# Feed-forward down stage: operand loads issued from ScalarE's step loop instead of SyncE's

## The chip, the cores and the metric

One Trainium2 chip, one core of it. The metric is the device time of one execution in microseconds (us), here the median of the runs of the same program.

## What is computed

One layer of a streaming encoder for 1152 tokens (1024 of a prompt, 8 x 16 of a sample), all in float32. The layer is: a half-step SwiGLU feed-forward network (`ffn`, called "f1"), a combined projection, sparse attention and an mLSTM branch with an output projection, and a second half-step SwiGLU network ("f2"), then a final norm. The change lies in `ffn` alone, which computes

```
a, b = split(rmsnorm(x, g) @ w_up)
x + 0.5 * ((silu(a) * b) @ w_down)        # D_MODEL 1024, D_FF 2816
```

and runs twice, once with each network's weights. Outputs that matter here are `y_prompt` and `y_sample`; the other outputs (keys, values, mLSTM state) do not depend on anything that is changed.

## The kernel before, in words

The program is written by hand for each engine: TensorE multiplies, ScalarE and VectorE evict and form operands, GpSimd forms the low halves of weights, SyncE issues every DMA. Every float32 product is three passes over split values (`product3`, L515: hi weight with lo activation, lo with hi, hi with hi), and every 2x2 block product of `ffn` is done with seven products instead of eight.

`ffn` (L522) is divided into tiles `n`: 22 up tiles (`UPS`) and 20 down tiles (`DOWNS`), and each tile into steps `q` (8 for the first two tiles, else 7). Steps are numbered through by `step(n, q)`: the up stage is steps 0 to 155, the down stage 156 to 295. TensorE (L1034 and on) takes one product per step, adds one to the semaphore `mm_ok` when it is done, and works through the steps in order. A step of the down stage has 12 matmuls of 288 columns (18 in the last round).

The activations between the stages don't fit in the on-chip memory as they are needed. For each pair of up tiles (a group `g`, eleven of them), seven combinations are split into hi and lo in a small ring of three staging buffers `stg` and stored to the DRAM tensor `h_dram`. ScalarE makes the hi half (`pack_hi`, L798), VectorE the lo half (`pack_lo`, L969), SyncE stores it (`store`, L721), and ScalarE may fill a staging buffer again only when its last store has landed (L805). The seven packs of the last group fall in steps 151 to 161, so across the border of the stages.

The down stage reads them back. It has five rounds of four tiles; round `r` works on the groups `ROUNDS[r]` (two groups, three in the last round), and its seven operands `xd[r, q]` are each loaded whole by `load_operand(r, q, s)` (L703), one DMA of 576 KB per group. A table `LOAD_AT` (L577) says at which step a load stands in the program: round 0 at steps 150 to 153 (two operands at 150, 151 and 152, one at 153), first used at steps 156 to 162; later rounds one operand every three steps through the round before, with first use 22 to 28 steps after (round 1: steps 156, 159, 162, and so on, first use 184 and on); the last three operands of the last round, with three DMAs each, at 262, 263 and 265, first use 272, 273 and 274. A load waits for `mm_ok` to reach its last argument (the step that freed the memory it overwrites), for the same operand of the round before, and for the stores of the groups that it reads.

What orders the other engines at each step `s`:

- SyncE (L729 to L737): raw weights for a later tile (`load_raw`, L692, which waits for GpSimd's progress on weights), then stores, then operand loads, then a residual load. It has no wait per step: it goes through the list and stops only where one of these calls waits.
- ScalarE (L853 to L857): `evict` (up stage only), then `split_hi` (L744) of the weight slot that this step frees, which waits until TensorE is done with step `s`, then `rest` (L821), in which `pack_hi` stands. A weight slot that is split at step `s` is multiplied at step `s + 4`; there are four slots.
- GpSimd (L867): the lo half of each weight slot, after the hi half.
- VectorE (L984 on): `evict`, which in the down stage is `accumulate` (L908: a PSUM pair added into `xT`), then `pack_lo`, `combine` (L954), and the differences of weights (`weight_term`, L875). TensorE may use a PSUM bank again only after `accumulate` has emptied it (`free_bank`): for step 160 that is the accumulation of step 158.

Of the kernel before, what the change touches and what calls it, by code (L numbers as in the profile page):

```python
# [16 lines left out]
F32 = mybir.dt.float32  # L17
# [504 lines left out]
def ffn(nc, ctx, M, K, w_up, w_down, gain, xT, xT_at, places, h_dram, r_dram, tag, first, last_io=None):  # L522

    sem = lambda n: ctx.enter_context(nc.semaphore(tag + n))
    UPS, ROUNDS = 2 * NG, ((0, 1), (2, 3), (4, 5), (6, 7), (8, 9, 10))
    DOWNS, RING, STG = 4 * len(ROUNDS), 4, 3
# [5 lines left out]
    def step(n, q):  # L532
        return 8 * n + q if n < 2 else 16 + 7 * (n - 2) + q

    def slot_no(n, x):
        return 4 * n + x if n < 2 else 8 + 7 * (n - 2) + x
# [35 lines left out]
    LOAD_AT = {}  # L572
    for r in range(len(ROUNDS)):
        for q in range(7):
            at, size = OPERAND[r, q]
            s = max(u[2] for u in used if u[0] < at + size and at < u[0] + u[1])
# [4 lines left out]
    done_groups = lambda r: sum(len(x) for x in ROUNDS[:r + 1])  # L581

    with ExitStack() as mem, M.scope():
# [13 lines left out]
             for x in range(3)]  # L597
# [8 lines left out]
        xd = {(r, q): M.at(f"{tag}xd{r}{q}", [P, len(ROUNDS[r]), 2, HT], OPERAND[r, q][0], F32R)  # L606
              for r in range(len(ROUNDS)) for q in range(7)}
        ps = psum(nc, mem, tag + "ps", [P, 8, 512])
        w_in = [sem(f"w_in{x}") for x in range(2)]
        st = [sem(f"st{x}") for x in range(STG)]  # L610
        xd_in = [sem(f"xd_in{q}") for q in range(7)]
# [11 lines left out]
        def round_of(n):  # L623
            return ROUNDS[(n - UPS) // 4]

        def raw_of(n):
            if n < UPS:
                return raw_u[:, n % 2].rearrange("p (k n) -> p k n", k=KT)
            return raw_d[:, n % 2, 0:len(round_of(n)) * 4 * P].rearrange("p (k n) -> p k n", n=2 * P)
# [51 lines left out]
        def y_block(m, i):  # L681
            k, t = 2 * (m % 4) + (0, 1, 1, 0)[i], (0, 1, 0, 1)[i]
            return xT[:, k, t * HT:(t + 1) * HT]

        with nc.Block() as block:
            @block.sync
            def _(sp):
                def load_up(n):
                    at = (n // 2) * 2 * P + (D_FF if n % 2 else 0)
                    sp.dma_start(raw_of(n), up_v[:, :, at:at + 2 * P]).then_inc(w_in[n % 2], 16)  # L690

                def load_raw(n):  # L692
                    sp.wait_ge(lo_ok, slot_no(n - 1, 0))
                    if n < UPS:
                        load_up(n)
                        return
                    if n == UPS + 1:
                        sp.wait_ge(lo_ok, U_SLOTS)
                    gs, p = round_of(n), (n - UPS) % 4
                    sp.dma_start(raw_of(n), dn_v[:, 2 * gs[0]:2 * gs[-1] + 2, 2 * p * P:2 * (p + 1) * P])\  # L700
                        .then_inc(w_in[n % 2], 16)

                def load_operand(r, q, s):  # L703
                    sp.wait_ge(mm_ok, s)
                    if r:
                        sp.wait_ge(xd_in[q], 16 * done_groups(r - 1))
                    for x in range(STG):
                        sp.wait_ge(st[x], 16 * len(range(x, 7 * done_groups(r), STG)))
                    for kk, g in enumerate(ROUNDS[r]):
                        sp.dma_start(xd[r, q][:, kk].bitcast(F32), h_dram.ap()[g, q]).then_inc(xd_in[q], 16)  # L710

                def load_residual(e):
                    if e < 2:
                        sp.wait_ge(r_st, 16)
                        sp.wait_ge(pl_ok, 7 * NG)
                    else:
                        sp.wait_ge(ra_ok, 2 * (e - 1))
                    k = 2 * (e % 4) + e // 4
                    sp.dma_start(res[e % 2][:], r_dram.ap()[:, k]).then_inc(y_in[e % 2], 16)

                def store(g, i):  # L721
                    o = 7 * g + i
                    sp.wait_ge(pl_ok, o + 1)
                    sp.dma_start(h_dram.ap()[g, PACK[i]], stg[o % STG][:].bitcast(F32)).then_inc(st[o % STG], 16)

                load_up(0)
                load_up(1)
                sp.dma_start(r_dram.ap(), xT[:]).then_inc(r_st, 16)
                for s in range(STEPS):  # L729
                    if s in RAW_AT:  # L730
                        load_raw(RAW_AT[s])
                    for g, i in LO_AT.get(s, ()):
                        store(g, i)
                    for r, q, free in LOAD_AT.get(s, ()):
                        load_operand(r, q, free)
                    if s in REST_AT:
                        load_residual(REST_AT[s])  # L737
                if last_io is not None:
                    z.load(sp)
                    z.store(sp)  # L740

            @block.scalar
            def _(act):
# [54 lines left out]
                def pack_hi(g, i):  # L798
                    o, q = 7 * g + i, PACK[i]
                    if q in (0, 1, 6):  # L800
                        act.wait_ge(hm_ok, nth(g, {0: 0, 1: 1, 6: 3}[q]))
                    else:
                        act.wait_ge(c_ok, 4 * g + {3: 1, 4: 2, 2: 3, 5: 4}[q])
                    if o >= STG:
                        act.wait_ge(st[o % STG], 16 * (o // STG))  # L805
                    else:
                        act.wait_ge(norm.sl_ok, 6)
                    nc.scalar.activation(stg[o % STG][:, 0], parts_of(g, i)[:], ACT.Copy).then_inc(ph_ok, 1)

                def square(e):  # L810
                    m, i = DOWNS - 4 + e // 4, e % 4
                    act.wait_ge(dn_ev, 7 * m + SQ_STEP[i] + 1)
                    if e >= 4:
                        act.wait_ge(sum_ok, e - 3)
                    else:
                        act.wait_ge(pl_ok, 7 * NG)
                    t = (0, 1, 0, 1)[i]
                    dst = K["acc"][:, t * HT:(t + 1) * HT] if e < 2 else sq[e % 2][:]
                    nc.scalar.activation(dst, y_block(m, i), ACT.Square).then_inc(sq_ok, 1)

                def rest(n, q):  # L821
                    s = step(n, q)
                    if n == 0 and q in (2, 3):
                        norm.high(act, 1, 2 * q - 4, "B")
                        norm.high(act, 1, 2 * q - 3, "B")
                    if s in SUM_HI_AT:
                        e = SUM_HI_AT[s]
                        if e >= 6:
                            act.wait_ge(mm_ok, step(1, 5) + 1)
                        norm.sum_high(act, e)  # L830
                    for g, i in HI_AT.get(s, ()):
                        pack_hi(g, i)
                    if last_io is None and n >= UPS + DOWNS - 4:
                        m = n - (UPS + DOWNS - 4)
                        if m and q == 0:
                            square(4 * m - 1)
                        if q in (2, 5, 6):
                            square(4 * m + (2, 5, 6).index(q))
# [14 lines left out]
                for s, (n, q) in enumerate(AT):  # L853
                    evict(n, q)
                    if s in FREED:
                        split_hi(FREED[s])
                    rest(n, q)  # L857
# [2326 lines left out]
```

## Time and profile before

| what | value |
|---|---|
| median of 3 runs | 2536.09 us (2535.38 to 2536.65) |
| the profiled execution, its own time | 2538.52 us |
| its span, first to last instruction | 2536.7 us |
| mean granted TensorE clock | 0.983 |
| f1: up stage, first down matmul, last | to 527.7 us, 527.8 us, 778.9 us |
| f2: first down matmul, last | 2257.1 us, 2508.4 us |
| DMA queues in use | one for all DMAs that SyncE issues (358.72 MB), two that fetch instructions (2.74 MB) |

Times are microseconds from the start of the span. A line begins with the line of the kernel (L710), the engine (PE is TensorE, DVE is VectorE, ACT is ScalarE, POOL is GpSimd, SPq is SyncE's queue of instructions), the operation and the tiles written and read. In brackets stands how long the engine was idle before it and what ended that. "issue" is a wait whose end the profile does not show. PEclk is the granted clock of TensorE as a fraction of 2.4 GHz.

### The profile page before, as it was taken

What the parts mean: (1) busy time and instruction counts of PE and PEld (TensorE: products, weight loads), DVE (VectorE), ACT (ScalarE), POOL (GpSimd) and SP (SyncE); (2) the same over time, 40 slices, a digit from 0 to 9 for tenths busy, and PEclk for the clock granted to TensorE, in tenths of its full rate; (3) what the DMA queues carried; (4) which work ended last, traced back from release to release, by engine and by line L of the source; (5) the groups of instructions that cost most, each with busy time, mean ns of one, the idle gap of its engine ahead of it and who ended that gap; (6) DMA issues with size and microseconds to landing.
All of it is one profiled execution on the core that took longest, in us unless ns stands there. A gap on an engine that the chain in (4) does not pass through costs nothing. (4 is left out here: it accounts for less than half of the span.)

```text
span 2536.7 us, 43065 instructions
## 1 busy us (share of the span) xinstructions
PE 2469.3 (97%) x16970; PEld 2399.8 (95%) x16970; DVE 1651.9 (65%) x2570; ACT 992.5 (39%) x1875; POOL 914.1 (36%) x739
## 2 busy tenths in 40 slices
PE   7999999999998999999998999998999999999997
PEld 7999999999997989999997888998999999999997
DVE  8776766667765328998645653424867576667864
ACT  5444444422233332212557864323434344432223
POOL 1444444444455111212224103421344444444442
PEclk8999999999998999999998999998999999999998
DMA  5343343497634212112334422333234334487751
GB/s 211 114 149 131 140 149 136 152 360 280 261 133 142 64 54 79 52 52 85 100 90 100 60 58 89 126 108 125 89 136 161 127 136 144 144 320 287 292 190 75
DMA packets 227304, 361.47 MB, mean 142 GB/s; under 512 B 39644, under 2 KB 174872, under 8 KB 226720
## 3 DMA queue, kind: packets, MB, share of 16 engines
q1 hardware_dynamic: 227104, 358.72, 41.0%
q8 instruction: 135, 2.21, 0.4%
q14 instruction: 65, 0.53, 0.1%
HBM read 231.21 MB, written 126.26 MB: 141 GB/s over the span
## 5 line engine op out<-in xcount | busy, mean ns | idle before, releaser
L517 PE MATMUL f1ps<-f1xs_lo,f1w_hi 128*128 128x288 f32 x1248 | 369.0, 296 | 3.7 <-DVE f1xs_lo L417 3.7
L517 PE MATMUL f2ps<-f2xs_lo,f2w_hi 128*128 128x288 f32 x1248 | 368.3, 295 | 3.7 <-DVE f2xs_lo L417 3.7
L519 PE MATMUL f1ps<-f1xs_hi,f1w_hi 128*128 128x288 f32 x1248 | 369.2, 296 | 0.0
L519 PE MATMUL f2ps<-f2xs_hi,f2w_hi 128*128 128x288 f32 x1248 | 368.7, 295 | 0.0
L518 PE MATMUL f1ps<-f1xs_hi,f1w_lo 128*128 128x288 f32 x1248 | 368.6, 295 | 0.0
L518 PE MATMUL f2ps<-f2xs_hi,f2w_lo 128*128 128x288 f32 x1248 | 368.1, 295 | 0.0
L517 PE MATMUL d_ps<-xn_lo,d_w_hi 128*128 128x384 f32 x864 | 298.5, 345 | 6.9 <-POOL xn_lo L297 5.3
L518 PE MATMUL d_ps<-xn_hi,d_w_lo 128*128 128x384 f32 x864 | 293.6, 340 | 0.0
L519 PE MATMUL d_ps<-xn_hi,d_w_hi 128*128 128x384 f32 x864 | 293.5, 340 | 0.0
L517 PEld LDWEIGHTS f1ps<-f1xs_lo,f1w_hi 128*128 128x128 f32 x1248 | 235.1, 188 | 5.1 <-POOL f1w_lo L869 4.1
L517 PEld LDWEIGHTS f2ps<-f2xs_lo,f2w_hi 128*128 128x128 f32 x1248 | 234.7, 188 | 4.7 <-issue 3.9
L518 PEld LDWEIGHTS f1ps<-f1xs_hi,f1w_lo 128*128 128x128 f32 x1248 | 235.1, 188 | 0.1
L519 PEld LDWEIGHTS f1ps<-f1xs_hi,f1w_hi 128*128 128x128 f32 x1248 | 235.2, 188 | 0.0
L519 PEld LDWEIGHTS f2ps<-f2xs_hi,f2w_hi 128*128 128x128 f32 x1248 | 234.8, 188 | 0.0
L518 PEld LDWEIGHTS f2ps<-f2xs_hi,f2w_lo 128*128 128x128 f32 x1248 | 234.7, 188 | 0.1
L1565 POOL TENSOR_TENSOR d_w_lo<-d_raw,d_w_hi 128x1024 fp32r<-128x1024 f32 x36 | 86.4, 2399 | 406.6 <-ACT d_w_hi L1430 406.6
L517 PE MATMUL f1ps<-f1xd,f1dw_hi 128*128 128x288 f32 x616 | 182.7, 297 | 3.4 <-issue 2.8
L517 PE MATMUL f2ps<-f2xd,f2dw_hi 128*128 128x288 f32 x616 | 183.1, 297 | 3.0 <-issue 2.8
L1859 DVE TENSOR_SCALAR_CACHE_REDUCE sel_hits<-DM,sel_cand 128x1024 uint8<-128x1024 f32 (+6 forms) x217 | 184.9, 917 | 1.1
L519 PE MATMUL f2ps<-f2xd,f2dw_hi 128*128 128x288 f32 x616 | 183.2, 297 | 0.0
L518 PE MATMUL f2ps<-f2xd,f2dw_lo 128*128 128x288 f32 x616 | 182.7, 297 | 0.0
L519 PE MATMUL f1ps<-f1xd,f1dw_hi 128*128 128x288 f32 x616 | 182.6, 296 | 0.0
(416 smaller groups left out, 6069.1 us busy)
## 6 DMA issues: line engine op xcount, KB each, us to landing
h_dram<-f1stg SPq DMA_DIRECT2D x77, 576.0 KB, 3.3
f1xd<-h_dram SPq DMA_DIRECT2D x77, 576.0 KB, 8.0
h_dram<-f2stg SPq DMA_DIRECT2D x77, 576.0 KB, 3.3
f2xd<-h_dram SPq DMA_DIRECT2D x77, 576.0 KB, 8.1
f1raw<-in_w_ffn_up SPq DMA_DIRECT2D x22, 1024.0 KB, 6.4
f2raw<-in_w_ffn_up SPq DMA_DIRECT2D x22, 1024.0 KB, 6.4
d_raw<-in_w_in SPq DMA_DIRECT2D x35, 512.0 KB, 5.1
p_dram<-stage SPq DMA_DIRECT2D x24, 576.0 KB, 3.4
```

The costliest lines, as they stand in the source:

```text
L517: nc.tensor.matmul(out, w_hi, x_lo, start=first, stop=False, skip_group_check=onto)
L518: nc.tensor.matmul(out, w_lo, x_hi, start=False, stop=False, skip_group_check=onto)
L519: return nc.tensor.matmul(out, w_hi, x_hi, start=False, stop=final, skip_group_check=onto)
L1565: nc.gpsimd.tensor_tensor(w_lo[:, n0 % 2], raw[:, n0 % 2], w_hi[:, n0 % 2].bitcast(F32), ALU.subtract).then_inc(lo_ok, 1)
L1859: v.tensor_scalar(hits[:, off:off + L], views[j], limit, None, ALU.is_ge, ALU.add, accum_out=cnt[:, j:j + 1]).then_inc(cnt_ok, 1)
```

## The change

The function that begins an operand load is moved, with its waits and its place in the table of steps, from SyncE's program to ScalarE's. ScalarE calls it at the head of `rest`, behind `evict` and `split_hi` of the step and ahead of `pack_hi`. Stores, raw weights and residual loads stay with SyncE.

```diff
-                def load_operand(r, q, s):
-                    sp.wait_ge(mm_ok, s)
-                    if r:
-                        sp.wait_ge(xd_in[q], 16 * done_groups(r - 1))
-                    for x in range(STG):
-                        sp.wait_ge(st[x], 16 * len(range(x, 7 * done_groups(r), STG)))
-                    for kk, g in enumerate(ROUNDS[r]):
-                        sp.dma_start(xd[r, q][:, kk].bitcast(F32), h_dram.ap()[g, q]).then_inc(xd_in[q], 16)
...
-                    for r, q, free in LOAD_AT.get(s, ()):
-                        load_operand(r, q, free)
...
+                def load_operand(r, q, s):
+                    act.wait_ge(mm_ok, s)
+                    if r:
+                        act.wait_ge(xd_in[q], 16 * done_groups(r - 1))
+                    for x in range(STG):
+                        act.wait_ge(st[x], 16 * len(range(x, 7 * done_groups(r), STG)))
+                    for kk, g in enumerate(ROUNDS[r]):
+                        act.dma_start(xd[r, q][:, kk].bitcast(F32), h_dram.ap()[g, q]).then_inc(xd_in[q], 16)
+
                 def rest(n, q):
                     s = step(n, q)
+                    for r, q0, free in LOAD_AT.get(s, ()):
+                        load_operand(r, q0, free)
```

## Rows read from the trace of the kernel before

**Rows 1.** The profile's page: busy time of each engine.

```profile
PE 2469.3 (97%) x16970; PEld 2399.8 (95%) x16970; DVE 1651.9 (65%) x2570; ACT 992.5 (39%) x1875; POOL 914.1 (36%) x739
```

**Rows 2.** Waits of TensorE, 527 to 780 us: total, times, longest.

```profile
PE f1ps L517 <- issue: 2.8, 1, 2.8
PE f1ps L517 <- DVE xT L923: 0.5, 1, 0.5
```

**Rows 3.** Timeline of TensorE around its stalls, f1 and f2: start, duration.

```profile
537.13 0.37 PE L517 MATMUL f1ps<-f1xd,f1dw_hi 128*128 128x288 f32 x1 [2.78 <-issue]
...
547.43 0.37 PE L517 MATMUL f1ps<-f1xd,f1dw_hi 128*128 128x288 f32 x1 [0.47 <-DVE xT L923]
...
2266.36 0.58 PE L517 MATMUL f2ps<-f2xd,f2dw_hi 128*128 128x288 f32 x1 [2.78 <-issue]
```

**Rows 4.** Timeline of VectorE, 528 to 537 us.

```profile
528.09 0.75 DVE L903 TENSOR_TENSOR f1g<-f1g,f1ps 128x576 f32<-128x576 f32 x1 [1.32 <-PE f1ps L519]
528.76 1.19 DVE L972 TENSOR_TENSOR f1stg<-f1g,f1stg 128x576 fp32r<-128x576 f32 x1
...
530.55 0.74 DVE L972 TENSOR_TENSOR f1stg<-f1g,f1stg 128x576 fp32r<-128x576 f32 x1
...
535.42 0.94 DVE L890 TENSOR_TENSOR f1dts<-f1draw,f1dts 128x256 f32<-128x256 f32 x1
536.28 0.74 DVE L923 TENSOR_SCALAR xT<-f1ps 128x576 f32<-128x576 f32 x1
```

**Rows 5.** Busy time, count, PEclk and DMA share in three windows.

```profile
538.00:542.00 4.00, 4.00 (x21) 3.87 (x19) 3.71 (x6) 1.78 (x4) 2.03 (x3) 0.57 1.03 417
2266.00:2272.00 6.00, 5.64 (x23) 5.67 (x24) 5.72 (x9) 2.18 (x5) 3.14 (x3) 0.50 1.02 409
564.00:568.00 4.00, 4.00 (x32) 4.00 (x31) 3.12 (x6) 0.98 (x3) 2.01 (x3) 1.00 1.03 394
```

**Rows 6.** Timeline of SyncE's queue: start, time until the last of the group is issued.

```profile
508.93 4.94 SPq L710 DMA_DIRECT2D f1xd<-h_dram  x8
...
521.82 2.81 SPq L710 DMA_DIRECT2D f1xd<-h_dram  x2
...
702.59 3.09 SPq L710 DMA_DIRECT2D f1xd<-h_dram  x6
```

**Rows 7.** Operand loads issued 518 to 521.1, 521.5 to 525 and 551 to 555 us.

```profile
L710 SPq DMA_DIRECT2D f1xd<-h_dram x4: 320/414/648, 519.0 to 520.4; - x4
...
DMA to landing us min/median/max: 8.0/9.8/11.6
...
L710 SPq DMA_DIRECT2D f1xd<-h_dram x2: 1312/1380/1448, 521.8 to 523.2; - x2
...
DMA to landing us min/median/max: 9.7/11.4/13.3
```

**Rows 8.** Timeline of ScalarE: border of the stages, then one step of the steady part.

```profile
512.18 0.63 ACT L751 ACTIVATE f1w_hi<-f1raw 128x512 fp32r<-128x512 f32 x1 [1.99 <-PE f1ps L519]
...
525.24 0.67 ACT L808 ACTIVATE f1stg<-f1g 128x576 fp32r<-128x576 f32 x1
528.10 0.42 ACT L751 ACTIVATE f1dw_hi<-f1dts 128x256 fp32r<-128x256 f32 x1 [2.18 <-PE f1ps L519]
528.42 0.67 ACT L808 ACTIVATE f1stg<-f1g 128x576 fp32r<-128x576 f32 x1
...
543.55 0.69 ACT L808 ACTIVATE f1stg<-f1g 128x576 fp32r<-128x576 f32 x1 [3.46 <-DMA h_dram<-f1stg]
...
563.73 0.42 ACT L751 ACTIVATE f1dw_hi<-f1draw 128x256 fp32r<-128x256 f32 x1 [1.17 <-PE f1ps L519]
```

**Rows 9.** Timeline of GpSimd: one weight slot at the border.

```profile
525.42 0.74 POOL L869 TENSOR_TENSOR f1dw_lo<-f1dts,f1dw_hi 128x256 fp32r<-128x256 f32 x1 [2.46 <-ACT f1dw_hi L751]
```

**Rows 10.** Stores to h_dram: issue to landing, 440 to 505, then 529 to 532 us.

```profile
DMA to landing us min/median/max: 2.8/2.8/2.8
...
DMA to landing us min/median/max: 7.7/7.7/7.7
```

## The prediction

> **What bounds the kernel now.** First the page's busy times: TensorE is busy 97% of the span, ScalarE 39% [rows 1]. So an edit can win only where TensorE stands still or runs slow near the operand loads, and ScalarE has room to issue DMAs. Next the waits of TensorE through f1's down stage: in 250 us it stands still once for 2.8 us and once for 0.5 us, no more [rows 2]. The timeline puts the long one just ahead of 537.13 us, and at 2266.36 in f2 with the same 2.78 us; the short one ends at 547.43 and f2 has none like it [rows 3]. Both are at the border of the stages; the stall is step 160, the fifth of the down stage.
>
> The profile calls the end of the long stall "issue", so I had to find its releaser. An operand that is still under way is the obvious suspect, for it would be this change's business. But the operand of step 160 is among the four loads issued from 519.0 to 520.4, and the slowest of them lands 11.6 us after its issue [rows 7], by 520.4 + 11.6 = 532.0, five microseconds ahead of 537.13. What does end there is VectorE's accumulation of step 158, 536.28 + 0.74 = 537.02, which frees the bank for step 160 [rows 4]. From 528.09, where TensorE let it start, to that end VectorE has no pause. So the stall is VectorE's backlog: packs, combinations and weight terms of the border. Operand loads don't stand in it.
>
> The stall costs more than its length. Behind it the granted clock reads 0.57 from 538 to 542 in f1 and 0.50 from 2266 to 2272 in f2, so about the lower of the levels (1.2 of 2.4 GHz), where 564 to 568 reads 1.00 with 32 matmuls in 4 us, 0.125 us each [rows 5]. In f1 21 matmuls instead of 32 are 11 x 0.125 = 1.4 us; in f2 23 instead of 45 (5.64 us) are 22 x 0.125 = 2.75 us. Stall and clock together: 4.2 us in f1, 5.5 us in f2.
>
> **The change, part by part.** It moves 77 DMAs in each network, with their waits, to ScalarE's program; nothing is computed differently.
>
> *SyncE without them.* It is never what TensorE waits for. Gain 0, nothing exposed.
>
> *Steady part (steps 162 on).* ScalarE splits one weight slot per step, 0.42 us, and then idles 1.17 us [rows 8]. Every third step it now issues two DMAs of 0.32 to 0.65 us, as on SyncE where the queue isn't full [rows 7]; I take 0.41, so 0.8 us. Six waits already satisfied go before them: the eight loads of 508.93 took 4.94 us to issue with a median near that 0.41, leaving about (4.94 - 8 x 0.41) / 4 = 0.4 us per operand. Sum 1.2 us, about the idle time. If each took 1.4 us, as the last two of the border [rows 7], ScalarE would be 2.8 + 0.4 - 1.17 = 2.0 us late. What covers that: a slot split after step s is multiplied at s + 4, three steps of 12 x 0.125 = 1.5 us later, 4.5 us, of which split (0.42) and GpSimd's part (0.74) [rows 9] need 1.2. That leaves 3.3 us. Price 0 for either value. For the last round three DMAs per operand are issued after step 262, 263 and 265 instead of from 702.59 [rows 6], a step later. The slowest landing in these rows is 13.3 us [rows 7]. From the end of step 265 to step 274 lie two steps of 1.5 us and six of 18 x 0.125 = 2.25, 16.5 us, and the other two have as much: price 0.
>
> *Start of round 0.* SyncE issued the first loads at 508.93, when step 149 was done [rows 6]. ScalarE reaches them behind the split of step 150, at 512.18 + 0.63 = 512.8 [rows 8]: 3.9 us later. "Begun in ScalarE's order" is here "begun later". The first is needed at 527.7, 15 us on: covered. The whole burst shifts, though. On SyncE the last two of the fourteen issues took 1.4 us each [rows 7], the time in which one load of 576 KB moves at the 417 GB/s of the saturated windows (0.59 MB / 417 GB/s = 1.4 us) [rows 5]: the queue took no more, and the issuer was held at the pace of the transfers. The last issue ended at 521.82 + 2.81 = 524.63 [rows 6]. On ScalarE it ends at 524.63 + 3.9 = 528.5 if the queue fills as before, and 1.4 + 1.3 us earlier, 525.8, if a store and a raw weight load that now have another queue leave room. I take the middle, 527.
>
> *What waits behind it.* ScalarE's split and pack of step 154, the pack from 525.24 to 525.91 before [rows 8], come at 527 to 528. GpSimd's part of the slot then ends by 528.3, and it is needed at step 158, two steps after 527.7, at 530.7: covered. The pack is needed by VectorE at 528.76 [rows 4]: covered by 0.8 us, or late by 0.7 at the upper bound. The next pack, 528.42 [rows 8], has till 530.55 [rows 4]. But GpSimd's part of the slot of step 154 now falls beside VectorE's backlog. A pack with GpSimd beside it took 1.19 us, one without 0.74 [rows 4]. So one more operation is 0.45 us longer and with it the stall. Bounds 0 and 0.45 + 0.7 = 1.15 per network; I take 0.45, from the nearest row, twice: +0.9 us.
>
> *Loads of round 1 at steps 156 and 159.* Four issues between packs, 0.4 to 1.4 us each, where ScalarE waited 3.46 us for a staging buffer anyway [rows 8]. Price 0; the upper bound is a rival.
>
> *Stores in a queue of their own.* A store landed after 2.8 us in quiet and 7.7 us behind the burst of operands [rows 10]. If stores pass the operands, the 3.46 us wait shrinks, VectorE's last packs move up, and the short stall of 0.47 us in f1 goes [rows 3]. Bounds 0 and -0.47; I take -0.47 since the difference of 4.9 us is more than the wait.
>
> A rule bears on this term. The Trainium skill, DMA: Bandwidth & Descriptors, "Issuing engines are not separate DMA queues", says that DMAs from different engines end up on the same 16 DMA engines and that several issuers save issue time only. By it this term would be 0 and the sum 0.5 us higher.
>
> Sum: 0 + 0 + 0.9 - 0.47 = **+0.4 us** against the profiled execution's own 2538.52 us, so 2538.9. The median of the runs lies 2.43 us below that execution, so I forecast a median of 2536.09 + 0.4 = **2536.5 us**.
>
> **The rivals.** About 0.2%, 5.1 us, is what a measurement of this kernel can tell from no change.
>
> *Slower: ScalarE is held at a full queue.* Place: steps 152 to 154. If ScalarE's queue holds fewer loads in flight than SyncE's did, or each issue there costs more, the last issue could end three loads later: 528.5 + 3 x 1.4 = 532.7. Then the pack for VectorE is at 532.7 + 0.4 + 0.6 = 533.7 instead of ahead of 528.76, VectorE stands still 4.9 us and step 160 comes 4.9 us later in each network; the clock behind it is low already and gives no more back. +9.8 - 0.5 gives 2545.4 us. It decides from a last issue later than about 527.8, and passes 0.2% at 530.5. For it: the 1.4 us rows are measured. Against: the burst is the same fourteen loads. The skill's Perfetto Trace Analysis, "DMA Instruction — HWDGE (DVE, Sync)", says that the issuing sequencer locks the descriptor generator and is free only when its descriptors are made; by that a full queue does hold ScalarE; no row here shows ScalarE issuing. Chance 0.16.
>
> *Faster: the overlap moves the other way.* The loads of step 156 hold back a later weight slot, GpSimd works less beside VectorE, two of the operations of rows 4 shrink by the 0.45 us between its two packs, and the shorter stall leaves the clock high. Then both networks win 0.9 us of stall and the 1.4 and 2.75 us of clock: -(1.8 + 4.15 + 0.47) = -6.4 gives 2529.7. Against: two thirds of the stall remain. Chance 0.07.
>
> *The stall is an operand after all.* Then a start 3.9 us later would lengthen it by up to 3.9 us twice, 2543.9. The landing rows speak against it; it is inside the slower chance.
>
> **How the numbers follow.** No change within 0.2%: 0.77, as all terms but those of the rivals are under 1 us. Slower 0.16, faster 0.07. The range, 2532.5 to 2543, leaves out the faster rival's full size and the upper half of the slower one.
>
> **What would show it.** Right: the first operand load near 512.8, the last of the burst by 528; two 2.8 to 3.3 us stalls of step 160 still ended by the accumulation; no stall after 560; store landings at the border under 6 us. Wrong: issues on ScalarE over 1 us in the steady part, a stall ahead of step 158, or VectorE waiting for a pack at 528.76. A time under 2531 would mean that the operands or the queue did stand in the border's stall.

## The result, and the profile after

| | before | after |
|---|---|---|
| median of the runs shown together | 2536.56 us (6 runs) | 2544.72 us (6 runs, 2543.91 to 2546.78) |
| span of the profiled execution | 2536.7 us | 2544.7 us |
| down stage of f1, start of the first and of the last matmul of L517 | 527.8 to 778.6 us | 527.7 to 782.1 us |
| down stage of f2, the same | 2257.1 to 2508.3 us | 2259.8 to 2517.1 us |

The changed kernel is slower: ratio 1.0033, 95% interval 1.002 to 1.0046. The forecast was 2536.5 us with a range to 2543.0, so the time lies outside. The down stages take 3.6 us (f1) and 6.1 us (f2) longer, 9.7 us together; between and behind them 1.7 us come back, which leaves the 8.0 us of the span.

The page of the changed kernel: busy times, then the queues.

```profile
PE 2469.9 (97%) x16970; PEld 2399.4 (94%) x16970; DVE 1650.0 (65%) x2570; ACT 991.1 (39%) x1875; POOL 912.4 (36%) x739
...
q1 hardware_dynamic: 204928, 267.88, 31.7%
q10 hardware_dynamic: 22176, 90.84, 9.5%
```

No engine has more work than in [rows 1]; the loss is waiting. A second queue, q10, now carries the operands, 90.84 MB in 22176 packets. That is 4096 bytes on average; where q10 alone works (519 to 522 us) 32 of 283 packets are under 512 bytes, so the others, with the data, can be whole rows of 4608 bytes.

Where TensorE waits from 527 to 560 us, which answers to [rows 2]:

```profile
PE f1ps L517 <- issue: 2.8, 1, 2.8
PE f1ps L517 <- DVE xT L923: 1.4, 1, 1.4
PE f1ps L517 <- DVE xT L927: 1.4, 1, 1.4
PE f1ps L517 <- DMA f1xd<-h_dram: 0.9, 1, 0.9
```

and in f2, 2262 to 2300 us:

```profile
PE f2ps L517 <- DVE xT L927: 2.8, 1, 2.8
PE f2ps L517 <- issue: 2.8, 1, 2.8
PE f2ps L517 <- DVE xT L923: 0.4, 1, 0.4
```

The 2.8 us stall of step 160 is still there in both networks. New are 3.7 us in three stalls in f1, where 0.5 us stood before, and 3.2 us in f2, all behind step 160. In f2 the second 2.8 us stall also costs clock (time, PE, PEld, DVE, ACT and POOL busy, then PEclk, DMA share, GB/s):

```profile
2288.00:2292.00 4.00, 2.10 (x9) 2.13 (x10) 2.62 (x5) 0.73 (x3) 2.60 (x3) 0.63 1.03 405
2292.00:2296.00 4.00, 4.00 (x19) 4.00 (x19) 1.58 (x2) 0.42 (x1) 0.73 (x1) 0.52 0.81 317
```

28 matmuls in 8 us instead of 64 are 36 x 0.125 = 4.5 us, of which 1.9 us stand in the stall (it ends at 2289.90) and 2.6 us in the clock, at the lower of its two levels.

What released the new stalls shows on ScalarE and VectorE:

```profile
540.41 0.68 ACT L797 ACTIVATE f1stg<-f1g 128x576 fp32r<-128x576 f32 x1 [1.81 <-DMA h_dram<-f1stg]
...
545.44 0.69 ACT L797 ACTIVATE f1stg<-f1g 128x576 fp32r<-128x576 f32 x1 [4.04 <-DMA h_dram<-f1stg]
...
554.96 0.73 ACT L740 ACTIVATE f1dw_hi<-f1draw 128x256 fp32r<-128x256 f32 x2 [3.29 <-DMA h_dram<-f1stg]
```

```profile
546.16 0.76 DVE L972 TENSOR_TENSOR f1stg<-f1g,f1stg 128x576 fp32r<-128x576 f32 x1 [2.74 <-ACT f1stg L797]
...
554.96 0.43 DVE L890 TENSOR_TENSOR f1dts<-f1draw 128x256 f32<-128x256 f32 x1 [1.45 <-DMA f1draw<-in_w_ffn_down]
```

ScalarE waits 4.04 us for a staging buffer (3.46 in [rows 8]), and VectorE now stands 2.74 us for that pack, where it stood 0.76 us before; TensorE's 1.4 us ahead of 549.30 follow. The row of before:

```profile
544.27 0.76 DVE L972 TENSOR_TENSOR f1stg<-f1g,f1stg 128x576 fp32r<-128x576 f32 x1 [0.76 <-ACT f1stg L808]
```

Then both engines wait for raw weights. The ScalarE row names a store, but the weights of the third down tile were issued at 539.5 and landed 15.5 us later, at 555.0, which is the moment both engines go on. SyncE's rows for the weight loads issued at 539.5 and 552.5:

```profile
L700 SPq DMA_DIRECT2D f1draw<-in_w_ffn_down x1: 482/482/482, 539.5 to 539.5; - x1
...
DMA to landing us min/median/max: 15.5/15.5/15.5
...
L700 SPq DMA_DIRECT2D f1draw<-in_w_ffn_down x1: 383/383/383, 552.5 to 552.5; - x1
...
DMA to landing us min/median/max: 12.3/12.3/12.3
```

Before, the same two landed 8.8 and 9.4 us after their issue. In f2, where most of the loss is, the rows name the weights themselves (chain that ended last, then ScalarE and VectorE):

```profile
2272.00 15.57 DMA f2draw<-in_w_ffn_down
```

```profile
2287.59 0.72 ACT L740 ACTIVATE f2dw_hi<-f2draw 128x256 fp32r<-128x256 f32 x2 [4.72 <-DMA f2draw<-in_w_ffn_down]
```

```profile
2287.59 0.42 DVE L890 TENSOR_TENSOR f2dts<-f2draw 128x256 f32<-128x256 f32 x1 [2.87 <-DMA f2draw<-in_w_ffn_down]
```

VectorE's accumulation follows at 2289.01, and TensorE starts at 2289.90, behind the second 2.8 us stall. Before, these weights landed 8.2 us after their issue. So what is late at the border is mostly weights and stores. That they wait for the DMA engines is so far a reading, which the experiments try.

### The profile page after: what moved, and what is told of

It is laid out like the page before. It is cut to its first block and busy times, and to the rows that moved or that the text cites. A ratio compares the mean times of both kernels' runs of the same rounds, so it can differ in the third digit from the quotient of the medians.

```text
span 2544.7 us, 43065 instructions
## 1 busy us (share of the span) xinstructions
PE 2469.9 (97%) x16970; PEld 2399.4 (94%) x16970; DVE 1650.0 (65%) x2570; ACT 991.1 (39%) x1875; POOL 912.4 (36%) x739
## 3 DMA queue, kind: packets, MB, share of 16 engines
q10 hardware_dynamic: 22176, 90.84, 9.5%
## 5 line engine op out<-in xcount | busy, mean ns | idle before, releaser
L517 PE MATMUL f1ps<-f1xs_lo,f1w_hi 128*128 128x288 f32 x1248 | 368.9, 296 | 4.6 <-DVE f1xs_lo L417 4.6
L517 PE MATMUL f2ps<-f2xs_lo,f2w_hi 128*128 128x288 f32 x1248 | 368.3, 295 | 3.6 <-DVE f2xs_lo L417 3.6
L517 PE MATMUL d_ps<-xn_lo,d_w_hi 128*128 128x384 f32 x864 | 298.2, 345 | 6.8 <-POOL xn_lo L297 5.1
L517 PEld LDWEIGHTS f1ps<-f1xs_lo,f1w_hi 128*128 128x128 f32 x1248 | 235.0, 188 | 5.8 <-POOL f1w_lo L869 4.8
L517 PEld LDWEIGHTS f2ps<-f2xs_lo,f2w_hi 128*128 128x128 f32 x1248 | 234.7, 188 | 4.7 <-issue 3.9
L517 PE MATMUL f2ps<-f2xd,f2dw_hi 128*128 128x288 f32 x616 | 184.6, 300 | 5.9 <-DVE xT L927 2.8
L517 PE MATMUL f1ps<-f1xd,f1dw_hi 128*128 128x288 f32 x616 | 182.9, 297 | 6.6 <-issue 2.8
```

The lines of the kernel that those rows point to most:

```text
L517: nc.tensor.matmul(out, w_hi, x_lo, start=first, stop=False, skip_group_check=onto)
```

## The experiments

Three theories were set against each other. LATE: the operand loads begin later (at 512.17 instead of 508.93, 3.2 us), the DMA engines stand idle meanwhile, and the backlog they then work off, which lasts to about 568 us, is later by that. SHARE: in two queues the raw weights lose to the operands. HELD: ScalarE is held up by issuing. Each median stands with its ratio to the kernel before, run on the same chip.

**All loads on SyncE, but late.**

```diff
-                        load_operand(r, q, free)
+                        load_operand(r, q, max(free, s + 1))
```

(made in the kernel before, in SyncE's loop)

> All operand loads stay on SyncE's single queue, but each waits until the step at which it stands is done, which is when ScalarE begins it in the changed kernel (first load near 512.8 us instead of 508.9). Theory LATE (the later start leaves the DMA engines idle for 4 us and pushes the whole border burst back): about 2544, the loss of the change. Theory SHARE (in two queues the raw weights, in small packets and issued before some operands, lose bandwidth to the operands' big packets): 2536 to 2538, and the raw weights issued near 540 us land within 10 us. Theory HELD (ScalarE is held up by issuing): 2536.5.

Measured: 2546.39 us, ratio 1.0035 (1.0021 to 1.0048). One queue, no load on ScalarE, and the whole loss of the change or more. SHARE and HELD aren't needed for a loss of this size. The first load begins at 511.46, 2.5 us later than before. Two windows show the start, first of the kernel before, then of this one:

```profile
507.60:511.60 4.00, 4.00 (x32) 4.00 (x31) 0.00 (x0) 1.17 (x2) 1.99 (x2) 1.00 0.41 114
```

```profile
507.60:511.60 4.00, 4.00 (x32) 4.00 (x32) 0.13 (x1) 1.24 (x3) 1.33 (x2) 1.00 0.00 0
535.00:569.00 34.00, 27.58 (x192) 27.40 (x193) 22.53 (x33) 8.82 (x20) 14.08 (x18) 0.90 1.01 382
```

The engines move nothing in the four microseconds in which they had begun the burst, and later their share is 1.01 over 34 us, so that they have no time over to make it up. The same two windows of the changed kernel:

```profile
507.60:511.60 4.00, 4.00 (x32) 4.00 (x31) 0.00 (x0) 1.17 (x2) 1.82 (x2) 1.00 0.00 0
535.00:569.00 34.00, 28.38 (x196) 27.59 (x197) 23.66 (x35) 8.84 (x22) 15.26 (x18) 0.95 1.01 392
```

SyncE is also held in the kernel with all loads on it:

```profile
521.00 6.51 SPq L710 DMA_DIRECT2D f1xd<-h_dram  x2
```

Two issues take 6.5 us. They end at 527.5, and the next store begins at 529.34, no later than before (529.98), but lands after 11.4 us instead of 7.7:

```profile
L724 SPq DMA_DIRECT2D h_dram<-f1stg x1: 320/320/320, 529.3 to 529.3; - x1
...
DMA to landing us min/median/max: 11.4/11.4/11.4
```

That is at 540.7. ScalarE waits for it until 540.81, and VectorE for ScalarE's pack:

```profile
540.81 0.68 ACT L808 ACTIVATE f1stg<-f1g 128x576 fp32r<-128x576 f32 x1 [4.60 <-DMA h_dram<-f1stg]
```

```profile
541.52 0.76 DVE L972 TENSOR_TENSOR f1stg<-f1g,f1stg 128x576 fp32r<-128x576 f32 x1 [3.82 <-ACT f1stg L808]
```

TensorE then stands still 4.9 us in f1 (to 544.83) and 3.5 us in f2, behind step 160: 8.4 of the 9.2 us.

```profile
PE f1ps L517 <- issue: 7.7, 2, 4.9
```

The edit does one thing more than LATE needs: SyncE works in order, so each load that waits for its step also holds what stands behind it. The weights of the third down tile are issued at 544.12 instead of 541.38 (landing after 9.7 us). How much of the 9.2 us this makes isn't separated, but the 4.9 us stall doesn't need it.

**ScalarE, but early.**

```diff
                 for s, (n, q) in enumerate(AT):
+                    for r, q0, free in LOAD_AT.get(s, ()):
+                        load_operand(r, q0, free)
                     evict(n, q)
```

(and the two lines taken out of `rest`)

> ScalarE issues the operand loads ahead of the eviction and the weight split of the step, so that the first begins near 508.9 us as on SyncE, in the queue of its own. LATE: 2536 to 2537. SHARE: 2541 or more, raw weights of the second and third down tile still need over 12 us to land. HELD: 2544 or more, since the same issues now stand ahead of the eviction too.

Measured: 2540.11 us, ratio 1.0012 (1.0003 to 1.002). Moving the same issues within ScalarE's step takes about half of the loss away or more (2.9 us are left of 8.2 and, in the second measurement below, of 5.6), though they now stand ahead of the eviction: HELD falls. 2.9 us stay, so LATE isn't all. The weights of the second down tile, issued at 519.5, land in 14.6 us, over the 12 that SHARE had, where before it was 12.3; those of the third, issued at 540.8, in 10.1 us, under 12, yet above the 8.8 of before.

**Round 0 on one engine, the rest on the other.** The changed kernel, with SyncE taking `load_operand` for `r == 0` only, and the reverse.

> Round 0 is loaded by SyncE as before, rounds 1 to 4 by ScalarE. LATE: 2536 to 2537, the burst begins at 508.9. SHARE: 2538 to 2541, only the loads of round 1 compete with the raw weights from the other queue. HELD: about 2540, half of the issues at the border are ScalarE's.

> Round 0 is loaded by ScalarE, rounds 1 to 4 by SyncE as before. LATE: about 2544, the burst still begins 3.9 us later. SHARE: 2538 to 2542, the burst competes from its own queue but the loads of round 1 stand in line with the raw weights. HELD: about 2540.

Measured: round 0 on SyncE 2539.51 us, ratio 1.0009 (1.0 to 1.0018); round 0 on ScalarE 2544.2 us, ratio 1.0026 (1.0016 to 1.0036). The fourteen loads of round 0, a fifth of those moved, carry most of the loss (7.0 us); the other 63 cost about 2 us, of which a part may be chance. But the second kernel loses in another place than the changed one. Waits of TensorE in it, f1 and f2, and the landing of the last two loads of round 0, issued from 521.3:

```profile
PE f1ps L517 <- DMA f1xd<-h_dram: 3.1, 2, 2.4
PE f2ps L517 <- DMA f2xd<-h_dram: 2.4, 1, 2.4
...
DMA to landing us min/median/max: 19.6/21.5/23.4
```

Here it is operands of round 0 that come too late, 5.5 us in both networks. So its time agrees with what LATE forecast, but it isn't a clean proof of the backlog's cost to weights and stores: the late start in a queue of its own also costs directly, through the last operand.

**Round 1 eight steps later.** In three kernels: the changed one, the one with the early start, and the kernel before.

```diff
-            LOAD_AT.setdefault(max(s + 1, step(UPS + 4 * r - 4, 3 * q)) if r else s + 1, []).append((r, q, s + 1))
+            LOAD_AT.setdefault(max(s + 1, step(UPS + 4 * r - 4, 3 * q) + (8 if r == 1 else 0)) if r else s + 1, []).append((r, q, s + 1))
```

> The changed kernel with the seven operand loads of round 1 moved 8 steps later in the table (steps 164 to 182 instead of 156 to 174, first use still 184 and on). LATE (a backlog of the DMA engines at the border, in which raw weights and stores are late): the late start is still there but nothing follows it closely, raw weights issued near 540 us land in under 10 us, the stalls behind step 160 go, 2537 to 2539. If instead the late start itself costs (round 0 arriving late): 2543 or more.

> ScalarE issues ahead of the eviction (start as on SyncE) and round 1 is 8 steps later. Backlog theory: no queue is full behind 535 us, so that two queues cost nothing: 2536 to 2537, at or just below the kernel before. If two queues cost something by themselves (issue time on ScalarE): 2540 as with the early start alone.

> The kernel before with round 1 moved 8 steps later, one queue. Backlog theory: the waits for staging buffers and the 0.5 us stall go, 2535.5 to 2537; the 2.8 us stall of step 160, which is VectorE's backlog, stays in both networks. If the DMA backlog also stands behind that stall: 2531 or less.

Measured: the changed kernel 2537.11 us, ratio 1.0002 (0.9993 to 1.0011); with the early start 2534.69 us, ratio 0.999 (0.9981 to 0.9999); the kernel before 2535.84 us, ratio 0.9993 (0.9985 to 1.0002). In the changed kernel the start is as late as it was (511.54), and the loss is gone once the loads that aren't needed yet are out of the way. The weights of the third down tile in it:

```profile
L700 SPq DMA_DIRECT2D f1draw<-in_w_ffn_down x1: 570/570/570, 539.0 to 539.0; - x1
...
DMA to landing us min/median/max: 7.1/7.1/7.1
```

and the DMA share over the border, against 1.01 in the changed kernel:

```profile
535.00:569.00 34.00, 31.25 (x202) 30.64 (x203) 23.90 (x34) 9.25 (x21) 14.74 (x19) 0.85 0.80 296
```

So in the changed kernel the late start costs through the backlog and hardly by itself; TensorE still waits 0.9 us at most for an operand of round 0 there. The second kernel says the same of the two queues: with an early start and no backlog, the 2.9 us are gone. ScalarE's time for issuing, which is in it as before, doesn't cost them. The third also answers the prediction's question: with weights landing in 4.7 us and stores in 3.2, its 2.8 us stalls are still in both networks. They are VectorE's.

**Packets of the raw weights.** The weights of the down stage are read as four pieces of 1 KB per partition, the operands as rows of 4.5 KB. This edit reads the weights as rows of 4 KB.

```diff
+                    if len(gs) == 2:
+                        sp.dma_start(raw_d[:, n % 2, 0:D_MODEL], dn_v[:, 2 * gs[0] + p]).then_inc(w_in[n % 2], 16)
+                        return
```

The first four down rounds then multiply by other rows of `w_down`; the work is the same.

> The changed kernel with the raw weights of the first four down rounds read as whole rows of 4 KB instead of four pieces of 1 KB per partition, the same bytes (the products of the down stage are then of other weights; TensorE's work is the same). Theory PACKET SHARE (engines take turns between the two queues by packet, so 1 KB packets get a fifth of the bandwidth beside 4 KB ones): the raw weights issued near 539 us land in 10 us or less instead of 15.5, and the time falls by 1 to 4 us, to 2541 to 2543. If the landing is a matter of the backlog alone: 14 us or more, and 2544.

> Control of the packet size: the kernel before (one queue) with the raw weights of the first four down rounds read as whole rows of 4 KB, other weights and the same bytes. PACKET SHARE: in one queue a transfer stands in line whatever its packets, so 2536 to 2537.5, as the kernel before. If 4 KB rows are a gain by themselves (fewer packets): 2533 or less, and then the gain of the same edit in two queues proves nothing of the sharing.

> Early start on ScalarE and raw weights of the first four down rounds in rows of 4 KB (other weights, the same bytes). If the 2.9 us that the early start leaves are the sharing by packets: 2536 to 2538, level with the one-queue kernel with the same rows. If they are ScalarE's issue time: 2539.5 to 2541 as with the early start alone.

Measured: in the changed kernel 2540.11 us, ratio 1.0013 (1.0004 to 1.0022). That is 4.6 us below its first median and 2.8 us below its second, a little more than was expected; the interval touches both of its intervals, so the size of the gain is uncertain. In the kernel before 2536.56 us, ratio 0.9996 (0.9987 to 1.0005), no change. In the changed kernel the same load now reads:

```profile
L701 SPq DMA_DIRECT2D f1draw<-in_w_ffn_down x1: 492/492/492, 539.3 to 539.3; - x1
...
DMA to landing us min/median/max: 10.0/10.0/10.0
```

10.0 us instead of 15.5, with as many bytes in the same backlog (DMA share 0.99 from 535 to 569). In one queue the landing of these weights didn't change (8.8 us before, 9.1 us with the rows of 4 KB). So the weights landed sooner by larger packets only where two queues competed. What was won there was in part taken elsewhere: TensorE now waits 2.3 us in f1 for an operand of round 0 (0.9 us before).

The Trainium skill, DMA: Bandwidth & Descriptors, "Queues, rings and completion order", says that each DMA engine takes turns between the queues it has work for, by packet. These two runs agree with that, if a queue of small packets gets fewer bytes per turn. A packet is on that page a group of descriptors; whether it is what the profile counts as a packet no run here shows.

With the early start it gave 2538.93 us, ratio 1.0009 (0.9999 to 1.0018), where 2536 to 2538 or 2539.5 to 2541 would have decided. That kernel's load lands in 9.2 us instead of 10.1. Inconclusive: the 2 to 3 us that the early start keeps need the backlog, since they go with the later round 1, but whether packet size makes them isn't settled.

**Twice the same.**

> The changed kernel once more beside the others: 2543 to 2546 by every theory; the down tiles' second raw weights land 12 us or more after their issue.

> The same kernel as the one with the early start on ScalarE and round 1 eight steps later, a second time, to see whether its 0.1% stands: 2534 to 2535.5 if it does, 2536 to 2537 if it was chance.

The changed kernel again: 2542.89 us, ratio 1.0026 (1.0016 to 1.0036), a little under the low end of what was expected; the ratio lies inside the first interval. The weights issued at 539.4 and 550.7 landed after 13.7 and 13.2 us, over 12 as expected. Its runs spread from 2539.64 to 2548.21, and its stalls don't fall the same each time: behind step 160 they are 2.5 us in f1 in this profile, 3.7 us in the first. The kernel with early start and later round 1: 2535.09 us, ratio 0.999 (0.9981 to 0.9999), the same as the first time. It beats both kernels, by about 0.1% against the one before, twice with an interval that ends just short of 1.

## Why the prediction was wrong

Point by point, in the prediction's order.

*What bounds the kernel*: right. The long stall is VectorE's backlog, not an operand; it measured 2.77 or 2.78 us in both networks in the profile of every kernel here, with and without a DMA backlog behind it.

*Steady part, price 0*: right. An issue on ScalarE takes 0.33 and 0.46 us, the pair 0.81 us, and it runs beside the split, not after it. (The waits ahead of a pair are five, four in round 0, not six; nothing hangs on it.) Three steps of the changed kernel, splits and issues:

```profile
562.39 0.42 ACT L740 ACTIVATE f1dw_hi<-f1draw 128x256 fp32r<-128x256 f32 x1 [1.15 <-PE f1ps L519]
562.57 0.81 ACTq L817 DMA_DIRECT2D f1xd<-h_dram  x2
564.01 0.42 ACT L740 ACTIVATE f1dw_hi<-f1dts 128x256 fp32r<-128x256 f32 x1 [1.20 <-PE f1ps L519]
565.58 0.42 ACT L740 ACTIVATE f1dw_hi<-f1draw 128x256 fp32r<-128x256 f32 x1 [1.15 <-PE f1ps L519]
```

*Start of round 0*: the step that failed. "3.9 us later" was nearly right. It was 3.2 us, since the issue doesn't wait for the end of the split ahead of it:

```profile
512.02 0.63 ACT L740 ACTIVATE f1w_hi<-f1raw 128x512 fp32r<-128x512 f32 x1 [1.99 <-PE f1ps L519]
512.17 1.81 ACTq L817 DMA_DIRECT2D f1xd<-h_dram  x4
```

"Covered" held for the first operand but not for the last, for which TensorE waited 0.9 us. And "the whole burst shifts, though" was followed only to the issuer. I asked when each operand of round 0 is needed and how long ScalarE would be held, and priced at nothing what the DMA engines lose. They are a resource with a backlog here: the windows of [rows 5] read a share of 1.03 and 1.02 at the border and still 1.03 at 564 to 568, which I used for the clock and the rate alone. An idle stretch ahead of a full one is passed on to what stands behind it, here the weights of the next tiles and the stores that free the staging buffers. For that term, put at 0, the late start in one queue measured +9.2 us (with what stood behind SyncE's held loads in it) and the move of the start on ScalarE 2.8 to 4.6 us (2542.89 and 2544.72 against 2540.11); the rest up to the loss is what two queues cost in the backlog.

*What waits behind it*: wrong in both parts. The last of the fourteen loads was issued by 522.8, not 527; ScalarE was hardly held, and the splits and packs of steps 154 and 155 kept their times, so the +0.9 us never came.

```profile
521.72 1.06 ACTq L817 DMA_DIRECT2D f1xd<-h_dram  x2
```

But these two landed after 18.6 and 20.7 us, where the same two took 12.4 and 13.1 before: the issuer was let go early, and the transfers ended late. The 13.3 us that the prediction used as the slowest landing is that of a later group.

*Stores in a queue of their own*, -0.47 us: wrong in sign. The store of 539.1 landed after 9.0 us, where the one of 539.3 took 5.4 before, and the short stall grew from 0.5 to 1.4 us instead of going. I had reasoned that stores pass the operands; here they didn't. The rule of the Trainium skill, DMA: Bandwidth & Descriptors, "Issuing engines are not separate DMA queues", by which this term was 0, was nearer.

*The slower rival* had the size, 2545.4 us, and the wrong mechanism and place. ScalarE was not held at steps 152 to 154; the new stalls are behind step 160. Its size agreeing is chance. *The faster rival* didn't happen. *The operand after all*: not the 2.8 us stall, as said; behind it, 0.9 us in f1 are a small piece of the loss in the changed kernel, but with round 0 alone on ScalarE such waits made 5.5 us.

*What would show it*: of the signs named, the ones on ScalarE's issues came true and the ones on landings did not: store landings "under 6 us" were 9.0. That one line, looked up first, would have pointed at the DMA engines.

## What to carry to other kernels

When a DMA is begun later and its own first use is far off, look also at the share of the DMA engines around it: if they are full for long afterwards, the delay is passed on to whatever stands behind, and here urgent transfers paid it. Putting bulk loads in a queue of their own cost the issuing engine little here, but didn't protect the urgent queue, whose packets were smaller. Loads that aren't needed for twenty steps are best kept out of a stretch in which the engines are full; here that was worth the whole loss, and with the early start 0.1% more.

## What was not expected of the hardware

ScalarE's queue took fourteen loads of 576 KB without a long hold, the longest issue 1.08 us in f1, while in [rows 7] SyncE's last two took 1.3 to 1.4 us each, and 5.1 us for one in the kernel with the late start on SyncE. SyncE's queue also held stores and raw weights, in many more packets, but what sets the limit wasn't tried. In two queues the loads issued at 545.8 and 546.2 landed after 7.5 and 9.8 us, the first of them at 553.3, ahead of the weights issued at 539.5 (555.0): between queues a later transfer can end first. And the two losses don't add: the late start costs 9.2 us in one queue and the two queues 2.9 us with the early start, but both together 6 to 8 us.
